# Side projections spread over eight state-space groups, squares and scaling taken group by group

## The reference

```python
h = rmsnorm(x, norm1_g[l])
proj = h @ w_in[l]
q, k, v, z, xbc, dt_raw, gate_logits = jnp.split(proj, SPLIT_POINTS, axis=-1)
...
y_fwd = ssd_scan(xs, dt[:, :, 0], a_neg[0], bm, cm)
y_bwd = ssd_scan(xs[:, ::-1], dt[:, ::-1, 1], ...)[:, ::-1]
y = (y_fwd + y_bwd + d_skip[:, None] * xs).reshape(b, s, SSM_INNER)
m = rmsnorm(y * jax.nn.silu(z), norm_g)          # over 2048 features
m_out = m @ w_ssm_br[l]
g_att, g_ssm = jnp.split(jax.nn.sigmoid(gate_logits + gate_b[l]), 2, axis=-1)
x = x + (g_att * a_out + g_ssm * m_out) @ w_out[l]
x = x + peer_ffn(rmsnorm(x, norm2_g[l]), ...)    # 128 gathered expert rows a token
```

## Time and profile before

| | us |
|---|---|
| median of three runs | 2524.89 |
| lowest and highest run | 2520.98, 2525.39 |
| the profiled execution's own time | 2520.57 |
| its span, first to last instruction | 2518.8 |
| TensorE busy in the span | 2095.1 (83%) |
| DVE, ACT busy | 1328.7 (53%), 759.3 (30%) |
| mean granted TensorE clock | 0.982 of full |

### The profile page before, as it was taken

The page is one execution under the profiler, slowest core; times in us unless marked ns, Lnnn a source line. Parts: engine busy times, 40 slices in busy tenths (PEclk is TensorE's granted clock), DMA queues, the critical chain, the costliest instruction groups (busy, mean ns, idle before and its releaser), DMA issues.

```text
span 2518.8 us, 22116 instructions
## 1 busy us (share of the span) xinstructions
PE 2095.1 (83%) x7800; PEld 1313.9 (52%) x7800; DVE 1328.7 (53%) x3223; ACT 759.3 (30%) x2027; POOL 515.5 (20%) x550
## 2 busy tenths in 40 slices
PE   5989999989877777777788999989887777777776
PEld 5678888857322232222275888878662222322222
DVE  1266365313776666665404772661256676666644
ACT  2034246112332333233211431660123323333232
POOL 0000000001533333333200000000033333333331
PEclk9999999999999999999999999999999999999999
DMA  4323444246999999999732334423369999999996
GB/s 162 115 106 129 164 180 159 101 158 265 410 421 421 421 421 421 422 421 422 322 134 100 132 132 164 168 109 144 149 269 421 421 422 421 421 422 421 421 421 265
DMA packets 90399, 705.25 MB, mean 280 GB/s; under 512 B 10000, under 2 KB 10128, under 8 KB 15792
## 3 DMA queue, kind: packets, MB, share of 16 engines
q0 software_dynamic: 78400, 553.81, 53.2%
q1 hardware_dynamic: 11168, 146.36, 15.5%
q10 hardware_dynamic: 720, 3.67, 0.4%
HBM read 702.62 MB, written 1.18 MB: 279 GB/s over the span
## 4 chain that ended last, share of the span: by engine, by line
PE 51%; DMA 33%; DVE 8%; ACT 4%; issue 2%; POOL 2%; ACTq 0%; SPq 0%; DVEq 0%; POOLq 0%
DMA ring<-in_peer_uv,ex_i 33%; PE bank L385 22%; PE bank L618 7%; PE bank L370 7%; DVE ring L1244 5%; PE bank L586 4%; PE bank L567 2%; PE bank L412 2%; POOL ring L1323 2%; PE bank L542 2%; ACT diag L841 1%; PE bank L433 1%; PE bank L552 1%; PE bank L600 1%; PE bank L457 1%
## 5 line engine op out<-in xcount | busy, mean ns | idle before, releaser
L618 PE MATMUL bank<-ring,diag 128*128 128x512 f32 x2048 | 954.3, 610 | 318.4 <-ACT diag L841 318.4
L618 PEld LDWEIGHTS bank<-ring,diag 128*128 128x128 f32 x2048 | 372.4, 191 | 900.0 <-ACT diag L841 523.7
L1244 DVE SCALAR_TENSOR_TENSOR ring<-ring,h 128x1024 f32<-128x1024 f32 x512 | 607.2, 1223 | 442.4 <-DMA ring<-in_peer_uv,ex_i 442.3
L1323 POOL DMA_INDIRECT ring<-in_peer_uv,ex_i x512 | 496.7, 970 | 1099.3 <-PE bank L618 659.3
L385 PE MATMUL bank<-hT,w_ring 128*128 128x256 f32 x2560 | 565.3, 381 | 2.4 <-ACT hT L643 2.4
L385 PEld LDWEIGHTS bank<-hT,w_ring 128*128 128x128 f32 x2560 | 483.5, 190 | 73.8 <-issue 7.0
L828 ACT ACTIVATE gel<-act_u 128x2 f32<-128x2 f32 x256 | 52.1, 203 | 856.7 <-DVE ring L1244 856.7
L841 ACT ACTIVATE diag<-cst,wgt 128x128 f32<-128x128 f32 x512 | 177.5, 394 | 8.4
L834 ACT ACTIVATE wgt<-gel,gate_w 128x1 f32<-128x1 f32 x512 | 122.9, 287 | 9.3
L1296 POOL DMA_DIRECT2D cs_rows_dram<-cs_rows x2 | 1.3, 663 | 600.4 <-DVE cs_rows L1022 600.4
L977 DVE SCALAR_TENSOR_TENSOR c_tmp<-xbc,par_all,c_tmp 128x254 f32<-128x254 f32 (+1 forms) x256 | 112.3, 480 | 4.6
(11 more groups left out here) (185 smaller groups left out, 1587.2 us busy)
## 6 DMA issues: line engine op xcount, KB each, us to landing
w_ring<-in_w_stream SPq DMA_DIRECT2D x68, 2048.0 KB, 7.7
fbuf<-cs_rows_dram POOLq DMA_DIRECT2D x32, 512.0 KB, 5.4
ring<-in_peer_uv,ex_i POOLq DMA_INDIRECT x512, 19.4
keys<-in_keys_t ACTq DMA_DIRECT2D x2, 1024.0 KB, 4.8
x_tok<-in_x SPq DMA_DIRECT2D x1, 1024.0 KB, 5.4
g2row<-in_norm_rows ACTq DMA_DIRECT2D x2, 512.0 KB, 5.7
out<-h SPq DMA_DIRECT2D x1, 1024.0 KB, 4.0
par_all<-in_params SPq DMA_DIRECT2D x1, 643.0 KB, 6.6
```

The costliest lines, as they stand in the source:

```text
L618: ins = pe.matmul(bank[b0 + n][:], diag[:, PAIR * (m % 2) + s, :], ring[:, slot, DM + n * 512:DM + (n + 1) * 512], start=False, stop=True, ...
L1244: ins = dve.scalar_tensor_tensor(out=row, in0=row, scalar=1.0, in1=h2[:, b, :], op0=ALU.mult, op1=ALU.mult, accum_out=act_u[:, b, PAIR * k ...
L1323: pool.indirect_dma_start(ring[:, PAIR * q + s, :], None, peer_uv, bass.IndirectOffsetOnAxis(ap=ex_i[:, b, j:j + 1], axis=0))\
```

## The change

The side projections become ten single halves: one ahead of the loop, one at the head of each of the 8 groups, one behind the loop. The squares of a group are taken on ACT one group later, from zT into the group's own tiles of xbc, which nothing reads any more; y_sq2 is gone. TensorE sums them into bank 7, two groups behind, two products (four recorded matmuls) at a time; the last two groups' are summed behind the tenth half. DVE scales zT by the gain two groups behind, once the square has been read from it. m_scaled counts groups instead of one event. On ACT there is one aside a group, between the two pairs of exponentials, where there were two in each of five groups.

```diff
-                beside = [C_Z + 1, C_Z + 2, C_Z + 3, C_GSSM, C_GSSM + 1]
+                def beside(n):
+                    half(C_Z + 1 + n // 2, n % 2, M_Z + 2 + n)
+
+                def sum_squares(g):
+                    wait(ysq_ready, g + 1, L)
+                    for u in range(2):
+                        ins = pe.matmul(bank[7][:, 0:SEQ], ones, xbc[:, 2 * g + u, :],
+                                        start=(g == 0 and u == 0), stop=(g == GROUPS - 1 and u == 1))
+                    ins.then_inc(ysq_used.sem, 1)
+
+                beside(0)
                 for g in range(GROUPS):
                     p = g % 2
-                    if g < len(beside):
-                        half(beside[g], 0, M_Z + 2 + 2 * g)
+                    beside(g + 1)
                     if g + 1 < GROUPS:
                         c_times_b(g + 1)
                     pe.wait_ge(m_ready.sem, m_ready.at(L, g + 1))
...
                     ins.then_inc(y_done.sem, 1)
-                    if g < len(beside):
-                        half(beside[g], 1, M_Z + 3 + 2 * g)
-
-                for i in range(XT // 2):
-                    wait(ysq_ready, i + 1, L)
...
-                wait(m_scaled, 1, L)
+                    if g >= 2:
+                        sum_squares(g - 2)
+                beside(GROUPS + 1)
+                sum_squares(GROUPS - 2)
+                sum_squares(GROUPS - 1)
+                wait(m_scaled, GROUPS, L)
...
+                def squares_of(g):
+                    wait(yz_ready, g + 1, L)
+                    act.activation(xbc[:, 2 * g:2 * g + 2, :], zT[:, 2 * g:2 * g + 2, :], ACT.Square)\
+                        .then_inc(ysq_ready.sem, 1)
+
+                aside(M_Z + 2)
                 for g in range(GROUPS):
                     if g + 1 < GROUPS:
                         cross_exps(g + 1, 4)
                         block_exps(g + 1, (0, 1))
-                    if g < 5:
-                        aside(M_Z + 2 + 2 * g)
+                    aside(M_Z + 3 + g)
                     if g + 1 < GROUPS:
                         cross_exps(g + 1, 5)
                         block_exps(g + 1, (2, 3))
                         cross_cb(g + 1)
-                    if g < 5:
-                        aside(M_Z + 3 + 2 * g)
...
+                    if g >= 1:
+                        squares_of(g - 1)
+                squares_of(GROUPS - 1)
+                aside(M_Z + 11)
...
+                def scaled(g):
+                    wait(ysq_ready, g + 1, L)
+                    for t in (2 * g, 2 * g + 1):
+                        ins = dve.tensor_scalar(zT[:, t, :], zT[:, t, :], param("sng", t, 1), None, ALU.mult)
+                    ins.then_inc(m_scaled.sem, 1)
+
...
                     if g + 1 < GROUPS:
                         differences(g + 1, (2, 3))
                         decay_times_cb(g + 1)
+                    if g >= 2:
+                        scaled(g - 2)
                 skip_and_gate(GROUPS - 1)
...
+                scaled(GROUPS - 2)
+                scaled(GROUPS - 1)
+
+                wait(ysq_used, GROUPS, L)
+                dve.tensor_scalar(r_bc[:], bank[7][:, 0:SEQ], 1.0 / INNER, EPS, ALU.mult, ALU.add)\
                     .then_inc(yms_ready.sem, 1)
```

More of the change, by code:

```diff
@@ L190, in encoder_kernel @@
         s_tmp, a3 = place(temps, "s_tmp", [P, 4, SEQ])
-        y_sq2, _ = place(temps, "y_sq2", [P, 2, 2, SEQ])
         r_bc, _ = place(temps + 8192, "r_bc", [P, SEQ])
@@ L294, in encoder_kernel @@
         yrms_ready = sem("yrms_ready", 1)
-        m_scaled = sem("m_scaled", 1)
+        m_scaled = sem("m_scaled", GROUPS)
         peer_loaded = sem("peer_loaded", 32)
```

## The result

The changed kernel takes 2497.9 us (median of 6 runs, 2496.6 to 2500.0); the kernel before takes 2524.1 us beside it (6 runs). The ratio is 0.9899, 95% interval 0.9886 to 0.9911, so about 26 us or 1.0% less. The forecast was 2498 us. The profiled execution took 2497.63 us, with a span of 2495.8 us.

The account below looks back on a forecast made before the run. TensorE bounds the stretch from first side half to SSM output projection; filling its waits saves 13.3 us a layer, 26.6 us for two. 2520.57 us becomes 2494.0, plus 4.3 for the median: 2498 us, range 2491 to 2507 us.

Parts of the forecast that it names:

- The bound and the sum: First side half to SSM output projection: TensorE's pieces without waits take 105.2 us plus 0.2 us of boundaries, against 118.7 us.
- What the old stretch lost: Same stretch before the change: TensorE waited 8.5 us, groups 5 to 7 and tail uncovered; the rest laid to the clock.
- The ring: ACT and DVE, from a full bank to readiness for the next: 10.4 to 10.7 us, under TensorE's 11.5 us a group.
- The cover behind it: TensorE asks for a group's m_mat only after its next half and C times B: 6.2 us to spare.
- Rival A: ACT and DVE's ring becomes the bound through costlier table switches: 13.0 us a group, 2504 us in all; chance 0.12.
- Rival B: Refills of fbuf come too late for the shorter groups: at a 22 us landing 2545 us; chance 0.03.
- Rival C: Groups 5 to 7 covered but the loop's end not, about 5 us a layer stay: 2508 us; chance 0.06.
- the step behind it: After group 7: skip, gate, Square and scaling hide under the tenth half; without that cover they cost 3 us a layer.
- Rival D: The time saved in the stretch is lost again downstream, so nothing moves: 2525 us; chance 0.03.
- the carry to the whole: Everything behind the output projection is started by data, so the net 26.6 us for two layers reaches the total.
- What would show it: Profile signs: stretch about 105 us, no TensorE wait over 0.5 us, clock 1.00, last group 2.8 us, sums 0.87 us.

Follow-up runs that it names:

- the run with the spreading alone: Kernel before with only the ten side halves spread out; squares, sums and scaling stay at the end: 2499.6 us, ratio 0.9903.
- the loaded runs: Changed kernel with two, five or nine extra scratch copies on ACT ahead of each group's aside: 2498.2, 2519.2 and 2560.8 us.
- two copies: Changed kernel with two extra scratch copies on ACT in each group, 1.3 us in all: 2498.2 us, stretch 105.76 us a layer.
- five and nine copies: Changed kernel with five or nine extra scratch copies on ACT in each group: 2519.2 and 2560.8 us, stretches 114.5 and 134.7 us a layer.
- two slots: Changed kernel with two slots of fbuf instead of three: 2501.2 us, stretch 105.76 us a layer.
- two convolution halves early: Changed kernel with two convolution halves moved ahead of the scores of attention head 1, later ones moved up: 2482.3 us, ratio 0.9830.

## Why the prediction was right

- **The bound and the sum.** TensorE without waits was to take 105.4 us a layer; it takes 105.8 us. Two terms were off in opposite ways. The sums cost 6 x 1.06 + 1.73 = 8.1 us, not 7.0: the first of them behind the y matmuls pays the boundary that otherwise the half pays. The halves cost 69.5 us, not 70.0: behind a sum a half takes 6.91 us, behind y matmuls 7.1 us. I had taken 0.2 us of boundary in all, and it is about 0.6 us. So the gain of a layer was 12.9 us for a forecast of 13.3 us.
- **What the old stretch lost** was misread in two places. The prediction laid the 7.66 us of the old sums to the clock. The granted clock over them was 1.00; their weight loads waited three times for the Squares, 1.0 us, two pieces in a buffer, as in the run with the spreading alone:

```profile
455.47:463.12 7.65, 7.65 (x33) 5.77 (x34) 6.13 (x19) 4.94 (x7) 0.00 (x0) 1.00 0.00 0
```

  The clock's part is in the y matmuls of groups 6 and 7. And it counted groups 5 to 7 as uncovered, but the y matmuls of group 5 began at 433.47 us straight behind C times B, since the second half of group 4 had covered them; the waits of the earlier trace rows all stand ahead of groups 6 and 7:

```profile
433.47 0.44 PE L542 MATMUL bank<-m_mat,x_fwd 128*64 128x128 f32 x4
```

  Neither reading enters the forecast, which takes the sum of TensorE's new pieces from the old stretch as measured.
- **The ring.** Forecast 10.4 us for the ring, 0.8 to 1.1 us of idle ahead of an aside. Measured 10.14 us by the loaded runs, and idles of 1.0 to 1.4 us ahead of the asides. The cover behind it was put at 6.2 us; at the last group, where it decides, the loaded runs show 5.0 to 5.1 us.
- **Rival A** did not happen, and its size is now known: a ring of 11.46 us (two copies) costs nothing in a group of 11.6 us, what a longer one adds up to is covered for the first 5 us, and then each us costs about 7 us a layer (20.2 us for 2.65 us between five and nine copies, 1.7 us of them the clock). A drain of 1.38 us on both switches would make it 12.9 us, by the same count a loss of about 5 us a layer; that is an estimate.
- **Rival B** was even less likely than the 0.03 given: two slots would have done.
- **Rival C**, an end that is covered only in part, did not happen. But the step behind it was mis-sized: without its cover the end costs 0.7 us a layer, not 3 us, since the sums of groups 5 and 6 still run there.
- **Rival D**, and the carry to the whole: everything behind L369 moved with it, so the gain of the stretches came through. That the median fell on the forecast to 0.1 us is luck beyond that: single executions of one kernel differ by 4 us, and the gain forecast 0.8 us too large met a median of the kernel before that came out 0.8 us lower over six runs (2524.1 us) than over three.
- **The parts.** The prediction did not weigh them apart. The spreading is the change; the group-wise squares bring 2.7 us a layer alone and 0.55 us beside it.
- **What would show it**: all signs came but one, the sums in pairs of 0.87 us, which are 1.06 us behind y matmuls.

## What to carry to other kernels

Count what covers each pass of a pipelined loop, not the cover of the whole: ten pieces of side work, two to a group in the first five, left TensorE waiting ahead of the last two groups, with the work after the loop uncovered as well, and the same ten pieces, spread one to a group, hid all of it. Whether the partner engines can follow the shorter pass is a ring to be added up from rows, from the hand-over of a bank to the readiness for the next; loading that ring with known work measures its slack and its cover. Once one engine is the bound and never waits, moving its own small pieces about brings little more: 0.55 of 12.9 us here.

## What the runs showed of the hardware

- The clock's return after a 6 us pause differed in code that all the kernels share: granted clock 1.00, or 0.65 to 0.74, over the first 6.9 us of the routing projection, about 2 us each time. In most profiles both layers agreed; with two convolution halves early layer 1 had 1.00 and layer 2 had 0.67. A difference of 4 to 5 us between such kernels need not come from the edit's own place.
- A group of 128x256 matmuls pays some 0.2 us more behind the y matmuls (128*64 in the rows): four took 1.06 us behind them and 0.86 us between halves; a half took 7.1 us behind them and 6.91 us behind a sum.
- Square on ACT needs no table load behind Exp, and none behind Sigmoid either: in the changed kernel's last pass it follows the gate without a row between.

```profile
438.54 0.84 ACT L723 ACTIVATE gateT<-bank,par_all 128x256 f32<-128x256 f32 x2 [5.04 <-PE bank L384]
439.27 0.63 ACT L783 ACTIVATE xbc<-zT 128x512 f32<-128x512 f32 x1
```
